# A hybrid attention and state-space encoder layer on one core: the loop over head groups written out on all five engines, and the residual for the output projection loaded tile by tile

## What is computed

```
h += 0.5 * SwiGLU_1(rmsnorm(h))
P  = rmsnorm(h) @ w_in          # z | x,B,C | dt | q | k | v | forget | gate_ssm | gate_attn
o_ssm  = Mamba-2 SSD(z, conv(xBC), dt)      # 32 heads, 8 groups, chunked scan
o_attn = forgetting attention(q, k, v, log f)   # 16 heads, sample rows also see a cache of 512
h += (sigmoid(gate_ssm) * (o_ssm @ w_br_ssm) + sigmoid(gate_attn) * (o_attn @ w_br_attn)) @ w_out
h += 0.5 * SwiGLU_2(rmsnorm(h))
y = rmsnorm(h)
```

## Time and profile before

| | |
|---|---|
| median of 3 runs | 2096.26 us (2094.61 to 2098.03) |
| profiled execution, its time | 2092.61 us |
| its span | 2090.9 us |
| PE busy | 1994.6 us (95%) |
| DVE, ACT, POOL busy | 946.5, 746.4, 415.2 us |
| granted TensorE clock, mean | 0.987 |

### The profile page before, as it was taken

The page is one execution under the profiler, slowest core; times in us unless marked ns, Lnnn a source line. Parts: engine busy times, 40 slices in busy tenths (PEclk is TensorE's granted clock), DMA queues, the critical chain, the costliest instruction groups (busy, mean ns, idle before and its releaser), DMA issues. The chain is left out here.

```text
span 2090.9 us, 38653 instructions
## 1 busy us (share of the span) xinstructions
PE 1994.6 (95%) x14875; PEld 1940.1 (93%) x14875; DVE 946.5 (45%) x1621; ACT 746.4 (36%) x1352; POOL 415.2 (20%) x508
## 2 busy tenths in 40 slices
PE   5999999995999999999999999999999999999998
PEld 5999999994989988998899889999999999999997
DVE  4433433445565357535753674113444443343344
ACT  5221221233454445445544554333222322122123
POOL 1000000003644344424442443223100000000000
PEclk9999999997999999999999999999999999999999
DMA  5222222232224412431243124314433322222221
GB/s 137 74 83 78 80 82 80 70 104 69 69 77 124 130 41 78 129 125 49 69 137 118 53 84 148 108 44 152 130 98 110 89 77 94 81 80 81 81 65 61
DMA packets 224432, 190.19 MB, mean 91 GB/s; under 512 B 9904, under 2 KB 211712, under 8 KB 223136
## 3 DMA queue, kind: packets, MB, share of 16 engines
q1 hardware_dynamic: 219520, 173.53, 27.6%
q0 software_dynamic: 4224, 14.55, 2.1%
q10 hardware_dynamic: 544, 0.17, 0.0%
HBM read 168.89 MB, written 19.33 MB: 90 GB/s over the span
## 5 line engine op out<-in xcount | busy, mean ns | idle before, releaser
L1629 PE MATMUL ps<-xah,wh 128*128 128x296 f32 (+1 forms) x2352 | 521.9, 303 | 18.8 <-DVE xal L1243 9.9
L1629 PE MATMUL ps<-xah,wl 128*128 128x296 f32 (+1 forms) x2352 | 517.6, 301 | 0.0
L1629 PE MATMUL ps<-xal,wh 128*128 128x296 f32 (+1 forms) x2352 | 512.8, 299 | 0.0
L1629 PEld LDWEIGHTS ps<-xah,wh 128*128 128x128 f32 x2352 | 379.9, 190 | 22.7 <-issue 9.5
L1629 PEld LDWEIGHTS ps<-xal,wh 128*128 128x128 f32 x2352 | 382.3, 189 | 0.0
L1629 PEld LDWEIGHTS ps<-xah,wl 128*128 128x128 f32 x2352 | 380.1, 189 | 0.5
L771 POOL TENSOR_TENSOR wl<-raw,wh 128x512 fp32r<-128x512 f32 (+1 forms) x184 | 229.9, 1257 | 417.9 <-ACT wh L881 417.7
L1629 PE MATMUL ps<-xbh,wh 128*128 128x288 f32 (+1 forms) x1312 | 281.0, 295 | 1.0 <-DVE xbl L1243 1.0
L1629 PE MATMUL ps<-xbl,wh 128*128 128x288 f32 (+1 forms) x1312 | 281.3, 295 | 0.0
L1629 PE MATMUL ps<-xbh,wl 128*128 128x288 f32 (+1 forms) x1312 | 281.3, 295 | 0.0
L1237 DVE TENSOR_TENSOR wl<-raw,wh 128x2048 fp32r<-128x2048 f32 x85 | 194.9, 2292 | 117.5 <-ACT wh L873 91.2
(11 more groups left out here) (252 smaller groups left out, 2353.8 us busy)
## 6 DMA issues: line engine op xcount, KB each, us to landing
raw<-in_ffn_w_in_dram SPq DMA_DIRECT2D x88, 512.0 KB, 5.0
raw<-in_w_in_dram SPq DMA_DIRECT2D x80, 512.0 KB, 4.5
raw<-in_ffn_w_out_dram SPq DMA_DIRECT2D x32, 512.0 KB, 3.9
brow<-acs_rows SPq DMA_DIRECT2D x8, 1184.0 KB, 6.4
raw<-in_w_br_ssm_dram SPq DMA_DIRECT2D x16, 512.0 KB, 4.3
raw<-in_ffn_w_out_dram SPq DMA_DIRECT2D x16, 384.0 KB, 3.6
bias<-bias_rows SPq DMA_DIRECT2D x32, 160.0 KB, 4.3
os_spill<-yT SPq DMA_DIRECT2D x8, 592.0 KB, 3.0
```

What stands on the lines that cost most here:

```text
L1629: ins = pe.matmul(bank(b + a, half), w[:, slot, k, j * P:(j + 1) * P], x[:, k, a * half:(a + 1) * half], start=(k == 0 and w is wh and x i ...
```

## The change

On each of the five engines the hardware loop over passes 0 to 2 is replaced by a loop of the program that builds the kernel, so that the passes stand one after another with constants. And the residual comes back in 16 transfers, two for each of 8 tiles, each pair issued as soon as `x_ready` says that its tile of the buffer has been read; they report to four semaphores, one for each duo of the output projection, and DVE waits for a duo's semaphore just before it adds the duo's first tile, behind the `split`.

```diff
-        h_out, h_back = sem("h_out"), sem("h_back")
+        h_out, h_back = sem("h_out"), [sem("h_back%d" % n) for n in range(KT // 2)]
@@ sync
-            with looped(sp, 3, st.all(), MID_PER[:3] + [0, 0, 0]) as i:
+            for i in range(3):
                 mid(i, LOOP_STEPS)
@@ gpsimd
-            with looped(pool, 3, [chain, nsplit, hparts], [2 * TILES, 10, 30]) as i:
+            for i in range(3):
                 mid(i, LOOP_STEPS)
...
-            pool.wait_ge(x_ready, n + KT)
-            to = 0
-            for c0, c1 in KEPT:
-                pool.dma_start(G2["h"][:, :, to:to + c1 - c0], h_spill.rearrange("p (k t) -> p k t", k=KT)[:, :, c0:c1]).then_inc(h_back, 16)
-                to += c1 - c0
+            for k in range(KT):
+                pool.wait_ge(x_ready, n + k + 1)
+                to = 0
+                for c0, c1 in KEPT:
+                    pool.dma_start(G2["h"][:, k, to:to + c1 - c0], h_spill[:, k * TOK + c0:k * TOK + c1]).then_inc(h_back[k // 2], 16)
+                    to += c1 - c0
@@ scalar
-            with looped(act, 3, st.all() + [chain], MID_PER + [0]) as i:
+            for i in range(3):
                 mid(i, LOOP_STEPS)
@@ vector
-            with looped(dve, 3, [chain, nsplit, hparts], [48, 10, 30]) as i:
+            for i in range(3):
                 mid(i, LOOP_STEPS)
...
-            dve.wait_ge(h_back, 32)
             for n, s in enumerate((1, 0, 1, 0)):
                 split(1 - s)
                 for u in range(2):
                     m = 2 * n + u
+                    if u == 0:
+                        dve.wait_ge(h_back[n], 64)
                     add_to_h(m, 2 * (m % 4), False)
@@ tensor
-            with looped(pe, 3, st.all(), [10, 0, 0, MID_OUTS, MID_OUTS, 0]) as i:
+            for i in range(3):
                 mid(i, LOOP_STEPS)
```

## The result

The changed kernel takes **2073.49 us** (median of 4 runs, 2072.41 to 2074.41); the kernel before, run beside it, 2095.44 us (4 runs, 2092.34 to 2098.03). The ratio is **0.9899 [0.9886, 0.9911]**, 21.9 us less.

A forecast was written before the change was run, and what follows sets the result against it. PE, busy 1994.6 of 2090.9 us, was taken to bound the kernel. Savings of 7.8 + 2.0 + 6.0 = 15.8 us gave 2076.8 profiled, a forecast median of 2080.5 us, range 2075.5 to 2089.0.

The forecast's parts named there:

- The residual: Output projection, second duo: PE's 4.35 us wait and 1.7 us lost to lower clock behind it go, 6.0 us.
- The spare time: Output projection: DVE's subtraction would end at 1601.2, PE wants it at 1607.1, some 6 us to spare.
- Passes 1 and 2: Two taken back branches removed: 3.9 us kept at each, 7.8 us less; bounds 1.1 to 5.4 each.
- pass 3 already is what the change makes of passes 1 and 2: Pass 3, entered without a branch, as model: `otok` to `sfin` 112.63 us against 116.53 in pass 2, 3.9 us less.
- PE's 5.4 us a branch: At each of two back branches: 3.7 us of PE idle plus 1.7 us lost to lower clock; 1.5 given back.
- Pass 0: Pass before any taken branch, also made of constants: 2.0 us less, pass 3 as model; bounds 0 and 2.0.
- the register instructions cost nothing I can find: Loop body in the passes: register instructions are worked off beside the matmuls, PE being 95% busy; no gain counted.
- the first rival: Scan: DVE and POOL share a port pair exclusively, so unrolling only moves their collisions; 6.5 to 9 us less, chance 0.12.
- The clock: Stretches at 1.2 GHz behind each back branch, in pass 0 and behind the residual's wait: 1.7 us lost in each.
- The scan takes it back: Passes 1 and 2: PE comes earlier, DVE and POOL do not, collisions return; 6.5 to 9 us less, chance 0.12.
- The residual's wait changes place: Output projection: a late tile or late high part of weights holds PE; only 9.8 us less, 2086.5, chance 0.05.
- Slower by code fetches: Written-out passes: late sequential fetches stop PE 5.4 us each; 65 us more if one in three late, chance 0.02.

The follow-up runs named there:

- wait_moved: Kernel before with its two large residual transfers kept, only DVE's wait moved behind the subtraction to the first addition: 2092.74 us, ratio 0.9998.
- pe_only: Kernel before with only PE's loop over the passes written out: 2091.02 us, ratio 0.9988.
- dve_only: Kernel before with only DVE's loop over the passes written out: 2091.86 us, ratio 0.9993.
- tiles_only: Kernel before with loops kept, only the 16 tile-wise residual transfers and the four moved waits added: 2086.49 us, ratio 0.9969.
- after_again: The changed kernel run and profiled once more, against the kernel before: 2073.09 us, ratio 0.9901.
- single_pass: Kernel before with three hardware loops of one pass each instead of one of three; these were turned into constants: 2079.44 us, ratio 0.9933.
- unroll_all: Kernel before with all five engines' loops written out, residual loaded as before: 2079.26 us, ratio 0.9931.
- others: Kernel before with the loops of ACT, POOL and SP written out, those of PE and DVE kept: 2089.81 us, ratio 0.9983.
- pe_dve: Kernel before with the loops of PE and DVE written out, those of ACT, POOL and SP kept: 2089.99 us, ratio 0.9989.
- pe_dve_act: Kernel before with the loops of PE, DVE and ACT written out, those of POOL and SP kept: 2086.42 us, ratio 0.9964.

## Why the prediction fell short

**The residual, forecast 6.0, measured 6.0.** 675.6 - 669.7 gives 6.0 us after the passes. The wait of 4.35 us went, and with it the fall of the clock behind it (window from 1590 above, clock 1.00). The spare time held. The number is right, the reading of the wait only in part. "PE has no weights" names one of two things that PE needs there. The other is a free result buffer, and that one came last: in before the weights are ready at 1608.34 + 2.29 = 1610.6, the first addition ends some 0.7 us later, and PE goes on at 1611.45, which is what "<-DVE h L1278" in the earlier trace rows says.

```profile
1610.55 1.42 DVE L1278 SCALAR_TENSOR_TENSOR h<-ps,h 128x576 f32<-128x576 f32 x2
```

So the wait moved behind the subtraction, the first of the edit's two parts, is worth nothing by itself (wait_moved); the transfers in pieces do the work.

**Passes 1 and 2, forecast 2 x 3.9 = 7.8, measured 4.1 + 4.8 = 8.9.** This is the first step that failed: "pass 3 already is what the change makes of passes 1 and 2". From `otok` to `sfin` pass 2 takes 0.9 us less than that model, and pass 3 itself, where it has no stretch of lower clock, is 0.9 us shorter in the changed kernel (below). Pass 1 came out at 112.7 us, as the model said, but with a stretch in it. The forecast gave back 1.5 of PE's 5.4 us a branch for engines that fall behind. Where a pass has no stretch (202.80 and 202.74 us in the table) it is 5.0 and 4.8 us shorter than in before: some 4.9 us a branch, of which 3.7 are PE's idle time, so 0.5 us is missing from the 5.4 and not 1.5. Clean, the two passes gain 412.0 - 404.9 = 7.1 us. A reason that fits is that the others need not fall behind, since they stop too. The forecast named DVE's stop and left out ACT's, which is not to be seen in the trace of before, and it gave neither a price. By the runs neither PE's nor DVE's loop alone is worth more than the 1 us that profiles differ by in these passes (clean: pe_only 413.0, dve_only 411.0, against 412.0); ACT, POOL and SP together give 2.0 and PE and DVE together 2.2; PE, DVE and ACT together (406.3) win 5.7 of the 7.1 us. ACT alone, or with only one of the two, was not tried.

**Pass 0, forecast 2.0, measured 3.2**, and **pass 3, forecast 0, measured about 0** (243.83 and 243.89). This is the second step: the form of the body was put at nothing ("the register instructions cost nothing I can find"). Pass 0 is entered without a taken branch in either kernel, so what it gains clean, 200.0 - 198.5 = 1.5 us, comes from the form of its body; only 2.0 - 1.7 = 0.3 of the forecast was that, the rest was the clock. Without a stretch on either side it is 200.26 (tiles_only) - 198.51 = 1.8 us. Whether register instructions are the part of the form that costs is not shown. PE's waits in pass 0 that the profile lists fell from 6.6 to 5.5 us in sum. The longest addition of DVE in the scan, though, is gone. DVE's `y` and `yg` over the whole span, in nanoseconds least/median/most, before and after:

```profile
L1519 DVE TENSOR_TENSOR y<-y x40: 420/426/2589, 569.6 to 1270.9; 128x256 f32<-128x256 f32 x32, 80x256 f32<-80x256 f32 x8
L1523 DVE SCALAR_TENSOR_TENSOR yg<-y,zs x40: 420/426/1373, 570.4 to 1271.3; 128x256 f32<-128x256 f32 x32, 80x256 f32<-80x256 f32 x8
```

```profile
L1520 DVE TENSOR_TENSOR y<-y x40: 420/426/1016, 566.7 to 1256.5; 128x256 f32<-128x256 f32 x32, 80x256 f32<-80x256 f32 x8
L1524 DVE SCALAR_TENSOR_TENSOR yg<-y,zs x40: 420/572/1949, 567.6 to 1257.0; 128x256 f32<-128x256 f32 x32, 80x256 f32<-80x256 f32 x8
```

The collision with POOL of the earlier trace rows has moved, not gone: in each pass it now meets `yg` (L1524), which takes up to 1.95 us, or `mb` with 2.02 us, and DVE's busy time over the span is 1.0 us more than before, not less. In this the first rival's rule held, without its price. Which of the two is met turns on hundredths of a microsecond. In pass 0 of after, DVE's L1520 starts at 577.38 and POOL's `xdd` at 577.41, and `yg` is the long one; in after_again they start at 579.60 and 579.63, POOL's gets longer (0.87 us) and `mb` is the long one.

Pass 3 was written out already. Without a stretch of lower clock on either side it is 243.83 - 242.93 = 0.9 us shorter (before, after_again); by the clean numbers of before and after it would be 1.6, but there one pass has a stretch (at 1174.5) and the other none, and clean it is as short as 242.7 in tiles_only, which keeps every loop. Why it gains 0.9 is not shown; it is entered from a pass in another form.

**The clock, a part of three terms.** The forecast had 6.8 us of it, 1.7 at each branch, in pass 0 and behind the residual's wait. Between 550 and 1700 us before's profile has four such stretches (from 583.8, 761.3, 969.5 and 1611.2), after's two, at other places (from 768.3 and 1174.5). Averaged over all runs, span x (1 - granted clock) is 29.2 us before and 23.8 after, so 5.4 us; the other 14.5 of the 19.9 us between the mean times, 2093.3 (57 runs) and 2073.4 (4 runs), match the clean passes, 7.1 + 1.5 + 1.6 = 10.2, and the wait of the residual, 4.35. The match is closer than the counting allows: single_pass, whose passes are those of unroll_all, loses 26.6 us by the same measure and unroll_all 24.5. Held against the forecast:

| term | forecast, us | measured, us |
|---|---|---|
| clean passes | 15.8 - 6.8 - 4.3 = 4.7 | 10.2 |
| wait of the residual | 4.3 | 4.35 |
| lower clock | 6.8 | 5.4 |
| sum | 15.8 | 19.9 |

The term that was mis-sized is the passes without the clock: passes 1 and 2 4.4 against 7.1, pass 0 0.3 against 1.5, pass 3 0 against 0.9 to 1.6.

**The base.** The forecast subtracted from the 3 runs' median of 2096.26. 57 runs of the same kernel average 2093.3 and lie between 2089.7 and 2096.6. That is 3.0 of the 7.0 us between forecast and result, the sum's 4.1 us the rest. The range had the same two faults: its low end put every term at its bound, but from that base, and its bounds had nothing for pass 3. From 2093.3 those bounds give 2093.3 - 18.9 = 2074.4.

**The rivals.** *The scan takes it back*: this is what happened in pe_only, where PE's stop became waits for others; with all five loops written out it fell. *The residual's wait changes place*: fell with the pieces; in wait_moved PE waits 3.8 us for the first addition, which came last in before too. *Slower by code fetches*: fell. The Trainium skill (Runtime: NRT & Kernel Launch, "Instruction fetch mechanics") says that code is fetched ahead strictly in sequence, and that a taken branch out of the pages held makes the engine wait for a fetch. The traces agree in that stops of 3.5 to 3.7 us on PE, 4.8 to 5.3 on DVE and 2.3 on ACT stand at the taken branch and none like them where the code runs on, and that more blocks are fetched at the branch. From 955 to 975 us of before there are

```profile
q8 instruction: 3, 0.05, 1.2%
...
q14 instruction: 4, 0.03, 0.6%
```

and from 945 to 965 us of the changed kernel only

```profile
q8 instruction: 1, 0.02, 0.4%
```

The stop also goes with the loop of its own engine: in pe_only q8, PE's queue of the earlier trace rows, fetches nothing from 963 to 975 us, around the second boundary, while q14 still fetches 4 blocks. That PE waited for just these blocks is an inference from their place; no run delays a fetch alone.

**Still open:** whether the last 1.4 to 2.3 us of passes 1 and 2 are a stop of POOL or SP or their register instructions; why a stretch of lower clock costs a pass less than the work lost in it; how the 1.5 us of pass 0 divide among the engines (clean, pe_only 199.5, dve_only 198.9, others 199.3, pe_dve 197.9, all 198.5: too close to part); and why pass 3 is shorter. The trial that was to part register instructions from branches did not, and no other was made.

## What to carry to other kernels

Here a taken back branch over a long body stopped three of the five engines that run the loop, PE, DVE and ACT, each for its own few microseconds, and these stops lie beside each other: price them together, look for the ones that another engine's lateness hides (a wait for that engine at one of the loop's first instructions), and do not expect a part of the engines to bring a part of the gain. Where a transfer must wait for a buffer to be read, cut it along the order in which the buffer comes free; moving the wait alone brought nothing here. When a wait is put down to one instruction, ask what else the engine needs there. And before a forecast stands on a few runs of the kernel, allow their scatter in the base itself, and do not take a neighbouring stretch as the model of the changed one without asking what it still carries from the old form.

## What the runs showed of the hardware that was not expected

- ACT stops at the taken branch as well, for 2.3 us, and this is invisible as long as DVE's stop of 4.8 to 5.0 us makes ACT wait at the same instruction (`th`, L1105).
- A stretch of lower clock in which 1.7 us of work is lost made a pass only 0.9 to 1.0 us longer in three comparisons of one kernel with itself; behind the passes the wait of 4.35 us and its stretch of 1.7 went for the full 6.0 us.
- Taking stops away can move the stretches of lower clock, not remove them: over all runs dve_only loses 33.4 us to them, before 29.2, pe_dve_act 30.8, after 23.8. That is why some kernels with shorter clean passes show nearly the time of before. In after, one such stretch lies in pass 1, at 768.3, 2 us behind a wait of PE of 0.87 us; what starts it was not tested.
- One transfer of 2 MB took 9.1 us to land in one kernel and 10.7 us in another, where eight of 256 KB took 3.0 us each (median), spread over other work.
